# Compression MLP, first layer: rows as the stationary operand in four 32-column groups, weights streamed

## The reference, cut to what matters

```python
def compress(x, pe, w1, b1, w2, b2):
    B_, S_, G_, d = x.shape                      # 1, 256, 2 groups, 128
    ch = x.reshape(B_, S_ // CMP_STRIDE, CMP_STRIDE, G_, d)
    blk = jnp.concatenate([ch[:, :-1], ch[:, 1:]], axis=2) + pe[None, None, :, None, :]
    nc = blk.shape[1]                            # 15 blocks of 32 positions
    flat = jnp.moveaxis(blk, 3, 2).reshape(B_, nc, G_, CMP_BLOCK * d)
    return jax.nn.gelu(flat @ w1 + b1) @ w2 + b2 # w1: (4096, 256), w2: (256, 128)
```

## Time and profile before

| what | value |
|---|---|
| median of 3 runs | 2120.5 us (2113.89 to 2121.41) |
| the profiled execution | 2111.32 us |
| its span, first to last instruction | 2109.6 us |
| PE busy | 1932.6 us, 92% of the span |
| DVE, ACT, POOL busy | 1556.3, 1051.4, 205.5 us |
| mean granted TensorE clock | 0.961 |
| DMA | 521.54 MB, mean 247 GB/s |
| chain that ended last | PE 77%, DVE 11%, DMA 7%, ACT 3% |

### The profile page before, as it was taken

How to read it: one execution, slowest core, us unless ns; L and a number is a source line. 1 busy time by engine, 2 the same in 40 slices (tenths; PEclk the granted TensorE clock), 3 DMA queues, 4 the chain that set the end, 5 groups by cost and what they waited for, 6 DMA issues and landing times.

```text
span 2109.6 us, 34759 instructions
## 1 busy us (share of the span) xinstructions
PE 1932.6 (92%) x11564; PEld 1670.9 (79%) x11564; DVE 1556.3 (74%) x2443; ACT 1051.4 (50%) x2269; POOL 205.5 (10%) x317
## 2 busy tenths in 40 slices
PE   3189979888999999999999899989999999999998
PEld 2068866566689999998777777768799999998787
DVE  4987752566878888888888878878777767678554
ACT  1145534545545555456444555555555545456443
POOL 2210000333100000000011000033000000000000
PEclk9689979899999999999999999999999999999999
DMA  8969976345668888886999686868667767665555
GB/s 328 412 253 340 316 257 188 135 161 186 238 232 269 279 266 281 281 268 211 330 335 342 221 298 194 279 222 298 219 232 223 224 203 243 202 204 177 177 189 177
DMA packets 210842, 521.54 MB, mean 247 GB/s; under 512 B 22897, under 2 KB 40818, under 8 KB 185874
## 3 DMA queue, kind: packets, MB, share of 16 engines
q1 hardware_dynamic: 180578, 316.17, 46.0%
q0 software_dynamic: 28032, 201.44, 26.1%
q10 hardware_dynamic: 2096, 2.12, 0.3%
HBM read 517.52 MB, written 2.12 MB: 246 GB/s over the span
## 4 chain that ended last, share of the span: by engine, by line
PE 77%; DVE 11%; DMA 7%; ACT 3%; issue 1%; SPq 0%; DVEq 0%; ACTq 0%; POOLq 0%
PE ps L1035 12%; PE ps L1031 11%; PE ps L1032 11%; PE ps L918 10%; PE ps L914 10%; PE ps L915 10%; DVE acc L1641 5%; DMA ring<-in_od_w_in 2%; DVE ring_lo L1719 2%; PE ps L1091 2%; PE ps L1083 1%; PE ps L753 1%; DMA aring<-in_ada_w 1%; DMA ring<-in_ev_w_in 1%; DMA first_ring<-in_ada_w 1%
## 5 line engine op out<-in xcount | busy, mean ns | idle before, releaser
L1205 ACT ACTIVATE ring_hi<-ring 128x512 fp32r<-128x512 f32 (+1 forms) x1152 | 688.5, 622 | 595.3 <-DMA ring<-in_ffn_w_up 248.4
L1719 DVE TENSOR_TENSOR ring_lo<-ring,ring_hi 128x512 fp32r<-128x512 f32 (+1 forms) x1152 | 741.8, 682 | 303.8 <-ACT ring_hi L1205 302.3
L1031 PE MATMUL ps<-hT_hi,ring_hi 128*128 128x256 f32 x2048 | 516.0, 284 | 5.7 <-issue 4.7
L1032 PE MATMUL ps<-hT_lo,ring_hi 128*128 128x256 f32 x2048 | 510.7, 281 | 0.0
L1031 PEld LDWEIGHTS ps<-hT_hi,ring_hi 128*128 128x128 f32 x2048 | 388.0, 189 | 7.0 <-issue 5.8
L1032 PEld LDWEIGHTS ps<-hT_lo,ring_hi 128*128 128x128 f32 x2048 | 390.3, 191 | 0.0
L1035 PE MATMUL ps<-hT_hi,ring_lo 128*128 128x256 f32 x2048 | 332.2, 283 | 5.2 <-issue 2.8
L1035 PEld LDWEIGHTS ps<-hT_hi,ring_lo 128*128 128x128 f32 x2048 | 281.6, 189 | 5.9 <-issue 3.3
L915 PE MATMUL ps<-ring_hi,hT_lo 128*128 128x512 f32 (+2 forms) x640 | 243.7, 382 | 0.0
L1641 DVE SCALAR_TENSOR_TENSOR acc<-aring,cs,acc 128x2048 f32<-128x2048 f32 x94 | 221.0, 2351 | 17.4 <-DMA aring<-in_ada_w 7.9
L637 POOL DMA_DIRECT2D aring<-in_ada_w x176 | 94.6, 538 | 1422.6 <-DVE acc L1641 1398.4
(11 more groups left out here) (234 smaller groups left out, 2053.0 us busy)
## 6 DMA issues: line engine op xcount, KB each, us to landing
aring<-in_ada_w POOLq DMA_DIRECT2D x176, 1024.0 KB, 6.7
ring<-in_ffn_w_up SPq DMA_DIRECT2D x512, 256.0 KB, 2.9
ring<-in_ffn_w_down SPq DMA_DIRECT2D x256, 256.0 KB, 3.1
ring<-in_od_w_in SPq DMA_DIRECT2D x112, 256.0 KB, 3.8
ring<-in_ev_w_in SPq DMA_DIRECT2D x96, 256.0 KB, 5.4
first_ring<-in_ada_w POOLq DMA_DIRECT2D x16, 1024.0 KB, 6.8
ring<-in_ev_w_out SPq DMA_DIRECT2D x64, 256.0 KB, 3.3
ring<-in_od_w_out SPq DMA_DIRECT2D x64, 256.0 KB, 4.3
```

The lines of the kernel that those rows point to most:

```text
L1031: nc.tensor.matmul(o[q], hi, hT_hi[:, kt, :], start=start, stop=False, skip_group_check=True)
L1032: nc.tensor.matmul(o[q], hi, hT_lo[:, kt, :], start=False, stop=False, skip_group_check=True)
L1205: ins = nc.scalar.activation(out_, in_, f, **kw)
L1719: put(v.tensor_tensor(ring_lo[:, g, part], ring[:, g, part], ring_hi[:, g, part].bitcast(F32), ALU.subtract), lo_ok)
```

## The change

The operands of the compression's first layer are swapped. For a position the stationary operand is now 32 columns of `flat` (30 rows of data and two more), and the 256 weight columns move. The result of position `at` goes to PSUM partitions 32 * (at % 4) to + 32 of bank 4 + a, so four consecutive positions use four column groups of the array. Each group adds up every fourth position. At the end ACT copies the 128 x 256 of partial sums to SBUF (`quarter`), and PE adds the four groups and turns the result back by two products with a constant of four stacked identities (`fold`), into bank 7, from which `hidden` reads. A 128 x 32 constant is loaded ahead for it, and DVE fills the two extra columns of `flat` with finite numbers (two copies of 128 x 64). In the late part `fold(1)` stands after block 4 and the second layer after block 5.

```diff
-        flat = side[:, 0:2 * CMP_BLOCK * 30].rearrange("p (a l r) -> p a l r", a=2, l=CMP_BLOCK)
+        flat = side[:, 0:2 * CMP_BLOCK * 32].rearrange("p (a l r) -> p a l r", a=2, l=CMP_BLOCK)
...
+        fold4 = wide[:, tail + 1430:tail + 1462]
+        quarters = L[:, :, :].rearrange("p b s -> p (b s)")[:, 1024:1536].rearrange("p (a n) -> p a n", a=2)
...
-            for dst, src in ((con[:, :], k_con), (hot, k_hot), (negrow, k_neg), (tbl, rel_bias),
+            for dst, src in ((con[:, :], k_con), (fold4, k_fold), (hot, k_hot), (negrow, k_neg), (tbl, rel_bias),
...
-            pe.wait_ge(params_in, 16 * 7)
+            pe.wait_ge(params_in, 16 * 8)
...
-                pe.wait_ge(flat_ok.handle, 8)
+                pe.wait_ge(flat_ok.handle, 10)
...
+                def fold(a):
+
+                    pe.wait_ge(quarter_ok.handle, a + 1)
+                    for hc in range(2):
+                        ins = nc.tensor.matmul(ps[:, 7, (2 * a + hc) * 32:(2 * a + hc) * 32 + NSA_G * NCMP],
+                                               quarters[:, a, hc * P:(hc + 1) * P], fold4[:, 0:NSA_G * NCMP], start=True, stop=True)
+                    lane.done(ins, fold_mm)
...
+                        if (kind, a, u) == ("cmp", 1, 8):
+                            fold(0)
...
-                                for hc in range(2):
-                                    ins = nc.tensor.matmul(ps[:, 4 + 2 * a + hc, 0:NSA_G * NCMP], w[:, l, hc * P:(hc + 1) * P],
-                                                           flat[:, a, 2 * u + l, :], start=(u == 0 and l == 0), stop=(u == 15 and l == 1))
+                                at = 2 * u + l
+                                rows_at = 32 * (at % 4)
+                                ins = nc.tensor.matmul(ps[rows_at:rows_at + 32, 4 + a, 0:CMP_HID], flat[:, a, at, :], w[:, l, :],
+                                                       start=at < 4, stop=at >= CMP_BLOCK - 4)
...
                 mix(MIX)
+                mix(MIX_LATE[:2])
+                fold(1)
+                mix(MIX_LATE[2:4])
                 pe.wait_ge(hid_ok.handle, 4)
...
-                mix(MIX_LATE)
+                mix(MIX_LATE[4:])
...
                 def hidden(a):
-                    act.wait_ge(unit_used.handle, mix_end("cmp", a, 15))
+                    act.wait_ge(fold_mm.handle, a + 1)
...
+                def quarter(a):
+                    act.wait_ge(unit_used.handle, mix_end("cmp", a, 15))
+                    run(quarter_ok, quarters[:, a, :], ps[:, 4 + a, 0:CMP_HID], ACT.Copy)
...
                     if (kind, u) == ("cmp", 15):
-                        hidden(a)
+                        if a == 1:
+                            hidden(0)
+                        quarter(a)
...
+                hidden(1)
                 act.wait_ge(kc_T.handle, 1)
...
+                for a in range(2):
+                    put(v.tensor_copy(flat[:, a, :, 30:32], con[:, C_COS64:C_SIN64].rearrange("p (l r) -> p l r", r=2)), flat_ok)
```

More of the change, by code:

```diff
@@ L122, in constants @@
     negrow = np.broadcast_to(np.where(j < S, 0.0, NEG).astype(np.float32), (SLOTS, REV))
-    return {"k_con": con, "k_hot": hot, "k_neg": np.ascontiguousarray(negrow)}
+    fold = np.tile(np.eye(32, dtype=np.float32), (4, 1))
+    return {"k_con": con, "k_hot": hot, "k_neg": np.ascontiguousarray(negrow), "k_fold": fold}
 class Signal:
@@ L195, in trunk_program @@
                   od_w_in, od_w_out, dsa_qk_g, ffn_w_up, ffn_conv_w, ffn_conv_b, ffn_w_down,
-                  k_con, k_hot, k_neg, out):
+                  k_con, k_hot, k_neg, k_fold, out):
     PLAN, SKIPPED = weight_plan()
@@ L380, in trunk_program @@
         sel_ok, ident_ok = sig("sel_ok"), sig("ident_ok")
+        quarter_ok, fold_mm = sig("quarter_ok"), sig("fold_mm")
         flipped, bias_ok = sig("flipped"), sig("bias_ok")
@@ L1459, in hidden @@
                 def hidden(a):
-                    act.wait_ge(unit_used.handle, mix_end("cmp", a, 15))
+                    act.wait_ge(fold_mm.handle, a + 1)
                     for hc in range(2):
                         col = ROWS["b1"][0] + 2 * a + hc
-                        run(hid_ok, hid[:, a, hc, :], ps[:, 4 + 2 * a + hc, 0:NSA_G * NCMP], ACT.Gelu_apprx_tanh, bias=prm[:, col:col + 1])
+                        run(hid_ok, hid[:, a, hc, :], ps[:, 7, (2 * a + hc) * 32:(2 * a + hc) * 32 + NSA_G * NCMP], ACT.Gelu_apprx_tanh,
+                            bias=prm[:, col:col + 1])
+                def quarter(a):
+                    act.wait_ge(unit_used.handle, mix_end("cmp", a, 15))
+                    run(quarter_ok, quarters[:, a, :], ps[:, 4 + a, 0:CMP_HID], ACT.Copy)
                 def mla_block(b):
```

## The result

| | before | after |
|---|---|---|
| median of the timed executions, same chip | 2118.48 us (2107.89 to 2124.78, 6) | 2095.19 us (2083.11 to 2114.41, 6) |
| the profiled execution | 2111.32 us | 2083.11 us |
| its span | 2109.6 us | 2081.4 us |
| mean granted TensorE clock in it | 0.961 | 0.966 |

The ratio is 0.9883 with an interval of 0.9845 to 0.992: 25 us faster, 17 to 33; the slowest of the six executions of the changed kernel, 2114.41 us, is over 1.5% above the fastest and left out of it. Of the 9 us between forecast and measurement 2 are those of the kernel before, whose median is 2118.5 in these six executions and was 2120.5 in the three that the forecast started from.

What follows compares the result with a forecast made beforehand. PE was taken to bound the mixer's first layer, with loads the next limit. 18.5 saved up to block 2, less 1.2, 0.2 and 0.5, gave 16.6 us: 2120.5 to 2104, range 2096 to 2112 (own bounds 2097 to 2110).

Steps and rivals of the forecast that it cites:

- The first layer itself: Compression's first layer on PE: four column groups side by side, 8.4 us at full clock in place of 33.5.
- The loads set T2: Mixer up to mla block 2: loads end later than PE's work (331.1 against 327.2), saving 18.5 us.
- T2: The end of mla block 2 on PE, forecast to move from 349.6 to 331.1 us.
- The walk of the loads: Sum of load times from 295.0 us: the last unit before block 2's end lands at 329.3.
- The tail gives back 1.2: Mixer after block 2: PE's block 6 waits 3.1 us for ACT's chain, ending at +23.1 instead of +21.9.
- the rival of the falling clock: Clock falls in the new idle before block 6: about 4 us back, 12.6 saved, 2108; chance 0.16.
- Small terms: DVE's two copies 0.2 us and the constant's load at the start 0.5 us, both as costs.
- its own bounds of 3, 1, 0.5 and 7 us: Forecast's uncertainties: load rate 3 us, tail 1, start 0.5, the runs' own spread 7, giving 2097 to 2110.
- An attention that starts 16 us earlier and ends less than 14 earlier: Sign named as proving the forecast wrong: layer 0's attention losing part of the earlier start.
- The loads did not keep up: Rival: compression loads as fast as mla loads, 0.69 us a unit; 20.5 saved, 2100; chance 0.12.
- The groups overlap: Rival claimed the opposite: first layer's column groups run in turn, 3.9 saved there, 2118; chance 0.05.
- The clock did not stay low: Rival claimed PE's waits for loads keep it at 1.2 GHz: 14 us slower, 2135; chance 0.04.

Runs made afterwards that it cites:

- after_b: The changed kernel unaltered, for a third profile; one execution, 2104.65 us.
- half_loads: The changed kernel with each compression unit loading 128 KB instead of 256, both its products using that half; 2091.87 us, ratio 0.988.
- block4_first: The changed kernel with ACT's copies and squares of mla block 4 ahead of the keys' squares and table load; 2097.64 us, ratio 0.9921.
- start_costs: The kernel before with only the constant's load, eight parameters to wait for, `flat` 32 wide and two DVE copies; 2112.05 us, ratio 0.9988.
- after_warm7: The changed kernel with seven instead of five warm products ahead of the attention; 2079.81 us, ratio 0.9828.
- attn_fill: The changed kernel with one added product behind the logits in each of the attention's first six steps; 2079.6 us, ratio 0.9831.

## Why the prediction was right or wrong

- **The first layer itself: right.** Four groups run side by side: 16 records in 1.07 us at full clock against a forecast of 0.88 and 0.2 for the changes of form. At 2.4 GHz the layer is forecast as 8.4 us; the group's busy time is 14.2 us and thus above the 8 to 11 forecast. A first run at half clock (2.00 us for 16 records) is a part of it: in after_b, with a first run at full clock, it is 12.6, and in half_loads, with that and fewer waits for loads, 9.7.
- **The loads set T2: right in kind, 2 us too small.** Block 2 is complete 38.0 us after the first product instead of 35.9, in all three profiles. The walk of the loads was right almost to the tenth: the last load before T2 lands 34.2 us after the first product (at 323.17), 34.1 were forecast. What was mis-sized is "its products take 1.8", one unit on PE behind that landing. The loads of the last pair land 0.7 us apart, PE comes to the pair only then, behind a run of the first layer, and the whole pair still has to run: it starts at 323.35 and takes 3.70. The load share of 0.91 to 1.07 was forecast as near 0.95, and the 290 to 380 GB/s too, though in the window read as "with mla loads" a compression load and one of 1 MB were still under way (DMA issues at 302.25 and 301.23, landed at 308.46 and 307.93). The gain up to block 2 is 16.3 us in the two first profiles and 15.6 in the means, against 18.5.

```profile
321.89 0.53 PE L1079 MATMUL ps<-wide,L 128*128 128x30 f32 x4
322.35 1.07 PE L1098 MATMUL ps<-ring,side 128*32 128x256 f32 x16
323.35 3.70 PE L1106 MATMUL ps<-ring,hT 128*128 128x512 f32 x8
```

- **The tail gives back 1.2: the wait right, its price too small.** The idle time before block 6 was put at 3.1 us and is 3.2 in all three profiles, put down to ACT, as forecast. But the clock fell at this place, and block 6 took 5.40, 6.36 and 6.43 us instead of 3.52. That is the rival of the falling clock, which had 0.16, in its place and at half to three quarters of its 4 us. The tail gave back 3.2 us (27.7 to 30.9), and 3.9 in the means. block4_first removed both.
- **Small terms: right or nothing.** start_costs cannot tell them from zero.
- **Local sum: 17.3 forecast (18.5 - 1.2), 11.7 to 13.1 measured.** Both terms of the mixer erred towards too large a gain.
- **The step that failed is the sum itself: that all other work keeps its time.** The mixer's 12 us lie 4 us below the nearer end of the gain's interval (0.9902, 16 to 26 us) and more below that of the first comparison. The prediction took 16.6 us for the whole from one stretch. In timed executions the changed kernel also spends some 29 us less at the lower clock outside the mixer, worth some 11 us; where and why is open. The range had 7 us for the runs' own spread and none for a clock that changes elsewhere; its own bounds of 3, 1, 0.5 and 7 us make 7.7 even if they are independent, not the 6 or 7 of "2097 to 2110". Two errors ran against each other, 4 to 6 us too much in the mixer and about 11 us left out outside it; that the time lies only just outside the range is luck, as without the first error the miss would have been larger.
- **What was named as refuting.** "An attention that starts 16 us earlier and ends less than 14 earlier" did not come in the first pair of profiles. It starts 19.3 earlier (358.0, where 361 was forecast, 6.2 of it from the program's start) and ends 26.0 earlier.
- **The rivals.** The loads did not keep up (block 2 at 38.0, not 32.0). The groups overlap. The clock did not stay low: it is 1.00 from 295 us on, though PE now waits for loads, and where PE ran 98% busy with 30-column products it had been 0.50.

One thing in the first list can't be taken as part of the cause: the start, 6.2 us shorter in the first pair. Over all profiles the stretch ahead of the layer, from the first column sums, is 181.5 to 185.7 us in the kernel before and 177.8 to 185.1 in the changed one; the two overlap.

Still open are the place and the cause of the 11 us outside the mixer, what makes PE pause in layer 1's up-projection, and whether the gains of half_loads and block4_first in the mixer, 4 and 3 us, reach the whole.

## What to carry to other kernels

With four positions in four column groups the products of the first layer take less than a third of what they take in turn (3.57 us for 16 records became 1.07), and the swap of operands without the groups gives the mixer nothing. Such a gain runs until the next limit, here the loads after some 16 us, and behind it a wait that was covered before (here ACT's table load ahead of block 6) can come to light: cost it, and the clock that may fall with it. At a limit set by loads, count what the engine still has to do when the last load lands; here it was a whole pair of units, not one. A gain of one per cent in a stretch is not yet the program's: hold the granted clock of many executions beside it before the whole is explained by one profile, and widen the range by what that clock moves.

## What the runs showed of the hardware beside this

- **The same instructions take 149.4 to 170.3 us.** Layer 0's attention, unchanged, differs by 21 us between executions of one kernel, with a granted clock of 0.93 and 0.82. One profile of each kernel can't find ten microseconds there.
- **The mean granted clock orders the executions.** 0.001 goes with 1.7 us in 74 executions of the kernel before, from 2103 us at 0.965 to 2130 at 0.955.
- **A loop of 3072 records differs by 14 us between programs in which it is the same.** Layer 1's up-projection takes 380 to 382.5 us in most kernels and 367.8 or 367.9 in three. The slow ones have four pauses of 1 to 3 us in it and a granted clock of 0.98 or 0.99, the fast ones none and 1.00. after_warm7 and attn_fill are by this the fastest kernels of the study, 2079.8 and 2079.6 us, ahead of the changed kernel by 12 to 15 us of medians, for a reason that isn't theirs by design.
- **Loads land later where PE uses them faster.** From issue to landing the compression's loads took 2.9 us at the median in the kernel before and 5.1 in the changed one.
